# Norms between the stages of a two-layer block: the row root from a folded sum, a seed and a Newton step

## The reference, cut to what matters

```
def rms_norm(x, w):
    x32 = x.astype(f32)
    y = x32 * lax.rsqrt(jnp.mean(x32 * x32, axis=-1, keepdims=True) + EPS)
    return (y * w.astype(f32)).astype(x.dtype)
```

## Time and profile before

| what | value |
|---|---|
| time, median of 3 runs | 2105.26 us (2105.2 to 2106.39) |
| span of the profiled execution, first to last instruction | 2104.1 us |
| PE busy | 2035.2 us, 97% |
| DVE busy | 1180.8 us, 56% |
| ACT busy | 779.2 us, 37% |
| mean granted TensorE clock | 0.989 of full speed |
| table loads on ACT | 40, 1283 ns each |

### The profile page before, as it was taken

One profiled execution on the slowest core, in us unless ns is written; L12 is line 12 of the kernel. 1 busy time (PEld: TensorE's weight loads), 2 busy tenths in 40 slices (PEclk: granted clock), 3 DMA queues, 4 the chain that ended last, 5 costly groups with the idle time before them and its releaser, 6 DMA issues.

```text
span 2104.1 us, 22893 instructions
## 1 busy us (share of the span) xinstructions
PE 2035.2 (97%) x9218; PEld 1570.5 (75%) x9218; DVE 1180.8 (56%) x1851; ACT 779.2 (37%) x1063; POOL 0.2 (0%) x4
## 2 busy tenths in 40 slices
PE   5999999899999998999999999999999999999997
PEld 3567666688888875657888888787877777888886
DVE  4224545575666467865756654456776855343434
ACT  4564444542322341154322323434343445232232
POOL 0000000000000000000000000000000000000000
PEclk9999979999999999999999999999999999999999
DMA  6112211145545314422555452211111122222221
GB/s 228 53 40 81 95 66 41 50 160 200 200 173 201 126 67 135 142 66 70 200 200 200 181 212 86 97 73 61 61 60 45 57 100 81 100 96 89 100 76 40
DMA packets 41345, 232.10 MB, mean 110 GB/s; under 512 B 6100, under 2 KB 7028, under 8 KB 15512
## 3 DMA queue, kind: packets, MB, share of 16 engines
q1 hardware_dynamic: 40856, 230.09, 29.8%
q10 hardware_dynamic: 384, 0.55, 0.1%
HBM read 219.84 MB, written 2.11 MB: 105 GB/s over the span
## 4 chain that ended last, share of the span: by engine, by line
PE 90%; DVE 5%; ACT 3%; issue 1%; DMA 0%; SPq 0%; DVEq 0%; ACTq 0%
PE ps L650 23%; PE ps L652 22%; PE ps L651 22%; PE ps L1108 2%; PE ps L698 2%; PE ps L861 2%; PE ps L883 2%; PE ps L1013 2%; PE ps L1141 1%; PE ps L683 1%; PE ps L687 1%; PE ps L867 1%; PE ps L684 1%; ACT L135 1%; PE ps L1129 1%
## 5 line engine op out<-in xcount | busy, mean ns | idle before, releaser
L650 PE MATMUL ps<-hh,wh 128*128 128x512 f32 x1378 | 561.7, 408 | 13.6 <-DVE hl L1821 5.1
L652 PE MATMUL ps<-hh,wl 128*128 128x512 f32 x1378 | 539.8, 392 | 0.0
L651 PE MATMUL ps<-hl,wh 128*128 128x512 f32 x1378 | 539.5, 392 | 0.0
L1792 DVE TENSOR_TENSOR wl<-raw,wh 128x2048 fp32r<-128x2048 f32 (+2 forms) x188 | 342.8, 1827 | 158.3 <-ACT wh L139 158.3
L139 ACT ACTIVATE wh<-raw 128x2048 fp32r<-128x2048 f32 (+2 forms) x168 | 284.7, 1698 | 329.0 <-PE ps L652 251.3
L650 PEld LDWEIGHTS ps<-hh,wh 128*128 128x128 f32 x1378 | 260.0, 189 | 86.2 <-issue 30.5
L652 PEld LDWEIGHTS ps<-hh,wl 128*128 128x128 f32 x1378 | 259.3, 188 | 56.6
L651 PEld LDWEIGHTS ps<-hl,wh 128*128 128x128 f32 x1378 | 259.9, 189 | 52.4 <-issue 3.4
L1848 DVE SCALAR_TENSOR_TENSOR xT<-ps,mod,xT 128x512 f32<-128x512 f32 x80 | 59.7, 749 | 161.2 <-PE ps L652 156.0
L652 PE MATMUL ps<-ffnHh,wl 128*128 128x512 f32 x256 | 99.6, 389 | 0.0
L652 PE MATMUL ps<-m0Hh,wl 128*128 128x512 f32 x256 | 99.6, 389 | 0.0
(11 more groups left out here) (369 smaller groups left out, 2725.9 us busy)
## 6 DMA issues: line engine op xcount, KB each, us to landing
raw<-in_m SPq DMA_DIRECT2D x64, 1024.0 KB, 4.9
raw<-in_ada SPq DMA_DIRECT2D x48, 1024.0 KB, 4.7
raw<-in_ffn SPq DMA_DIRECT2D x32, 1024.0 KB, 6.9
raw<-in_hin SPq DMA_DIRECT2D x20, 1024.0 KB, 4.8
raw<-in_win SPq DMA_DIRECT2D x11, 1024.0 KB, 6.6
raw<-in_cin SPq DMA_DIRECT2D x8, 1024.0 KB, 4.8
cus<-cu SPq DMA_DIRECT2D x112, 66.0 KB, 2.0
xT<-in_xT SPq DMA_DIRECT2D x16, 256.0 KB, 4.5
```

Source lines behind the costliest of these rows:

```text
L650: pe.e.matmul(out, wh[:, k, c], xh(k), start=i == 0, stop=False)
L651: pe.e.matmul(out, wh[:, k, c], xl(k), start=False, stop=False)
L652: t = pe.e.matmul(out, wl[:, k, c], xh(k), start=False, stop=i == n - 1)
L1792: t = dve.e.tensor_tensor(P.WL[p % NSPLIT][:, k, :], P.raw[n % NRAW][:, k, :], P.WH[p % NSPLIT][:, k, :].bitcast(F32), ALU.subtract)
```

## The change

The row sum and the root are computed in another layout, in all seven norms.

- Sum: in place of one 128x128 stationary of ones and 512 moving columns, four matmuls with 32 columns of ones each take 128 tokens each. Group g writes PSUM partitions 32g to 32g+31. The 512 sums then lie in 128 columns of the bank, tokens 128g to 128g+127 in band g. This is done for `nrm_acc` and again for the last square.
- Root: ACT takes a seed, `Abs_reciprocal_sqrt` of the 128 columns, into SBUF. DVE does a Newton step on it in three instructions of 128 columns, waiting for its own result between them. No Exp and no switch of the table stand in the norm; the table of `Abs_reciprocal_sqrt` takes the places where Ln's was loaded ahead.
- Spread: PE multiplies, four times, a stationary of 128x128 made of one column of `pick` (the factor -0.5/D in the first row of a band), read with stride 0, with the 128 columns. The result, the root on all partitions for 512 tokens, goes to bank 6.
- DVE's eight products read the root from that PSUM bank in place of `R` in SBUF.
- The six idle matmuls become two between the sum and the spread, and three after the spread.
- The first half of the early split is moved: on ACT to behind the seed, on DVE to behind the Newton step.
- SP's waits for the root or for `xn` become waits for the new semaphores at the same points.

```
 def pe_row_sum(pe, P, name):
-    Z, n = P.Z, NU[name] + 1
+    Z, n = P.Z, NU[name]
     b, before = P.banks.claim_mm(("row", name))
     pe.wait_ge(Z.evac[b], before)
-    pe.wait_ge(Z.acc, 6 * n)
-    pe.e.matmul(P.PS[b][:, :], P.ones, P.acc[:, :], start=True, stop=False)
-    pe.wait_ge(Z.sq, 8 * n)
-    pe.e.matmul(P.PS[b][:, :], P.ones, P.sq[1][:, :], start=False, stop=True).then_inc(Z.full[b], 1)
+    def fold(x, first):
+        for g in range(4):
+            t = pe.e.matmul(P.PS[b][32 * g:32 * g + 32, 0:128], P.ones[:, 0:32], x[:, 128 * g:128 * g + 128], start=first,
+                            stop=not first)
+        return t
+    pe.wait_ge(Z.acc, 6 * n + 6)
+    fold(P.acc, True)
+    pe.wait_ge(Z.sq, 8 * n + 8)
+    fold(P.sq[1], False).then_inc(Z.full[b], 1)
     if name in FIRST:
-        pe_idle(pe, P, name, 7, 6)
+        pe_idle(pe, P, (name, 0), 7, 2)
+    b, before = P.banks.claim(("root", name), 6)
+    pe.wait_ge(Z.evac[b], before)
+    pe.wait_ge(Z.pick, 1)
+    pe.wait_ge(Z.root, n + 1)
+    for g in range(4):
+        t = pe.e.matmul(P.PS[b][:, 128 * g:128 * g + 128], wide(P.pick[:, g:g + 1], [0, 128]), P.fold[2], start=True,
+                        stop=True)
+    t.then_inc(Z.full[b], 1)
+    if name in FIRST:
+        pe_idle(pe, P, (name, 1), 7, 3)
...
 def act_row_rsqrt(act, P, name):
     key = ("row", name)
     act.wait_ge(*P.banks.full(key))
-    act_rsqrt_of(act, P, key, 128, 1024)
+    act.act(P.fold[0], P.PS[P.banks.bank(key)][:, 0:128], ACT.Abs_reciprocal_sqrt, scale=1.0 / D,
+            bias=P.epst[:, :]).then_inc(P.Z.seed, 1)
...
 def act_norm(act, P, name, shift=None):
+    act_row_rsqrt(act, P, name)
     if name in P.early:
         act_split(act, P, P.early[name], 0)
-    act_row_rsqrt(act, P, name)
...
+def dve_root(dve, P, name):
+    Z, key = P.Z, ("row", name)
+    b = P.banks.bank(key)
+    seed, two, out = P.fold
+    stt = dve.e.scalar_tensor_tensor
+    dve.wait_ge(Z.seed, NU[name] + 1)
+    dve.did(stt(two, P.PS[b][:, 0:128], D * EPS, seed, ALU.add, ALU.mult))
+    dve.settle()
+    dve.e.tensor_tensor(two, two, seed, ALU.mult).then_inc(Z.evac[b], 1)
+    dve.wait_ge(*P.banks.evac(key))
+    stt(out, two, -3.0 * D, seed, ALU.add, ALU.mult).then_inc(Z.root, 1)
+    if name in P.early:
+        dve_split(dve, P, P.early[name], 0)
+    key = ("root", name)
+    dve.wait_ge(*P.banks.full(key))
+    return P.PS[P.banks.bank(key)][:, :], Z.evac[P.banks.bank(key)]
...
 def dve_norm(dve, P, name, gain, shift=None):
-    if name in P.early:
-        dve_split(dve, P, P.early[name], 0)
-    dve.wait_ge(Z.rs, RS[name])
+    root, free = dve_root(dve, P, name)
     for c in range(KC):
-        dve.e.scalar_tensor_tensor(P.sq[c % 2][:, :], P.xT[:, c, :], gain(c), P.R[:, :], ALU.mult,
-                                   ALU.mult).then_inc(Z.xn, 1)
+        t = dve.e.scalar_tensor_tensor(P.sq[c % 2][:, :], P.xT[:, c, :], gain(c), root, ALU.mult, ALU.mult)
+        t.then_inc(Z.xn if c < 7 else free, 1)
...
     dve_split(dve, P, 0)
     dve.wait_ge(Z.con, 32)
+    dve.e.tensor_scalar(P.pick[:, :], wide(P.ident[:, 0:1], [32, 4]), -0.5 / D, None, ALU.mult, ALU.bypass).then_inc(Z.pick, 1)
     dve_norm(dve, P, "mix", lambda c: V(P, "n1", c))
```

More of the change, by code:

```diff
@@ L23 @@
 TABLES = {ACT.Exp: "exp_and_others", ACT.Ln: "natural_log",
-          ACT.Sigmoid: "sigmoid_and_others", ACT.Silu: "silu_and_others"}
+          ACT.Abs_reciprocal_sqrt: "abs_reciprocal_sqrt_and_small", ACT.Sigmoid: "sigmoid_and_others", ACT.Silu: "silu_and_others"}
 NRAW = 4
@@ L337 @@
 RS = {n: i + 1 for i, n in enumerate((
-    "mix", "ffn", "conv", "var", "m0", "hgrn", "sc0", "sc4", "y7", "m1", "final"))}
+    "var", "sc0", "sc4", "y7"))}
 NU = {"mix": 0, "ffn": 1, "conv": 2, "m0": 3, "hgrn": 4, "m1": 5, "final": 6}
@@ L404, in allocate @@
         "values_half", "hout_used", "qsig", "f", "w", "gsig", "ds", "up", "os", "ns", "y7", "lbd", "lb", "sw"))
-    Z.xo, Z.eps = sem("x_out"), sem("eps")
+    Z.xo, Z.eps, Z.seed, Z.root, Z.pick = (sem(n) for n in ("x_out", "eps", "seed", "root", "pick"))
     P.xT = sb("xT", [128, KC, S])
@@ L418, in allocate @@
     P.R = sb("R", [128, S])
+    P.fold = [P.R[:, 128 * i:128 * i + 128] for i in range(3)]
+    P.pick = sb("pick", [128, 4])
     P.ident, P.ones, P.bd = P.con[:, 0:128], P.con[:, 128:256], P.con[:, 256:384]
@@ L1282, in act_norm @@
     Z = P.Z
+    act_row_rsqrt(act, P, name)
     if name in P.early:
         act_split(act, P, P.early[name], 0)
-    act_row_rsqrt(act, P, name)
     for c in range(KC):
-        act.wait_ge(Z.xn, 8 * NU[name] + c + 1)
+        act.wait_ge(*((Z.xn, 7 * NU[name] + c + 1) if c < 7 else P.banks.evac(("root", name))))
         x, h = P.sq[c % 2][:, :], P.hh[:, c, :]
@@ L1310, in act_ffn @@
         act.act(F.cb[:, :], F.cb[:, :], ACT.Silu).then_inc(Z.cond, 1)
-    act.load_table(ACT.Ln)
+    act.load_table(ACT.Abs_reciprocal_sqrt)
     for s in FFN_STEPS:
@@ L2397, in vector_program @@
     dve_ffn(dve, P, "m1", "final", lambda c: mcol(P, 1, 5, c))
-    dve.wait_ge(Z.rs, RS["final"])
+    root, _ = dve_root(dve, P, "final")
     for c in range(KC):
         x = P.xT[:, c, :]
-        dve.e.scalar_tensor_tensor(x, x, V(P, "fg", c), P.R[:, :], ALU.mult, ALU.mult).then_inc(Z.xo, 1)
+        dve.e.scalar_tensor_tensor(x, x, V(P, "fg", c), root, ALU.mult, ALU.mult).then_inc(Z.xo, 1)
 def sync_program(e, P):
@@ L2451, in sync_program @@
     dma(M.mc[:, 384:512], con("mc", 128)).then_inc(Z.mla, 16)
-    sp.wait_ge(Z.xn, 8)
+    sp.wait_ge(*banks.evac(("root", "mix")))
     dma(M.cs, con("cos", 2 * S)).then_inc(Z.mla, 16)
@@ L2474, in sync_program @@
         if P.slabs[n - NRAW] == ("cin", 1):
-            sp.wait_ge(Z.rs, RS["conv"])
+            sp.wait_ge(Z.root, NU["conv"] + 1)
             dma(C.wv[:, :, :, :], a["wv"]).then_inc(Z.taps, 16)
@@ L2481, in sync_program @@
         if P.slabs[n - NRAW] == ("hin", 1):
-            sp.wait_ge(Z.rs, RS["hgrn"])
+            sp.wait_ge(Z.root, NU["hgrn"] + 1)
             dma(H.msk[:, :, :], a["msk"]).then_inc(Z.mask, 16)
```

## The result

The changed kernel takes 2120.61 us (median of 4 runs, 2119.2 to 2121.63) against 2105.82 us for the kernel before on the same chip: a ratio of 1.0069, 95% interval 1.0056 to 1.0081. I had forecast 2102.0 and a range up to 2106.0. It is slower by 14.8 us, with the interval clear of 1, and the profiled execution has a span of 2117.4 us against 2104.1.

The account below looks back on a forecast made before the run. PE, busy 97% of the span, was taken to bound the kernel, gains coming only where it waits on the norms. Gains of 3.9 us less 0.6 in mix, net 3.3 from 2105.26, gave 2102.0 us; range 2099.0 to 2106.0.

Parts of the forecast that it names:

- forecast for ffn 0.3 gained: ffn's norm: PE's products start 5.1 us behind the last row sum in place of 5.39, gaining 0.3.
- conv and m0, 0.6 each: Norms of conv and m0: chain from row sum to DVE's first product falls from 3.83 to 3.22 us.
- hgrn 0.6, m1 1.2, together 1.8: hgrn's norm: chain from 3.83 to 3.22 us; m1's, with both sums on the path, from 4.66 to 3.47.
- final, 0.6: The final norm: chain from row sum to DVE's first product falls from 3.83 to 3.22 us.
- mix was to lose 0.6: mix's norm: `pick` and Newton step wait for DVE's split; DVE's product 0.8 us later, taken as 0.6 lost.
- the three idle matmuls: Behind the spread: they hold PE 2.0 us, to 5.1, so PE starts 0.25 late, unhidden in ffn.
- The folded sums didn't queue: Rival, all norms: narrow sums run one after another, each costing 0.6 us more; 2106.4 us, chance 0.12.
- mix didn't keep its clock: Rival, mix: the spread's work spares the half-clock stretch, up to 2.6 us come back; 2099.4 us, chance 0.14.
- No load stayed: Rival, all seven norms: a table load stays on each path, 9 us more; 2111 us, chance 0.04.
- Net 3.3 us ... 2102.0: Whole kernel: 3.9 us gained in six norms, 0.6 lost in mix, taken from the median 2105.26.
- The prediction's own sign for this case: DVE's product 0.6 us earlier in each norm without the time following: the chain's far end was read wrongly.
- a falling clock: Rival, norms other than mix: PE's idling halves the clock, 2.6 us a fall; five give 2115 us, chance 0.05.

Follow-up runs that it names:

- e10: e1 plus seven idle products filling PE's 2.97 us wait ahead of conv's third projection; 2102.33 us, ratio 0.9978 to the kernel before.
- e1: Changed kernel with `pick` in the unused bytes behind `epst`, so no other tile moves; 2105.07 us, ratio 0.9994 to the kernel before.
- e2: Kernel before plus one unused 32-byte-per-partition tile behind `R`, shifting later tiles; 2124.2 us, ratio 1.0086.
- e5: Kernel before with `Hl` moved 32 bytes in m0, `r` and `rs` 32 bytes in m1, nothing in ffn; 2112.22 us.
- e8: Kernel before, unchanged, run again for a second profile; 2105.95 us.
- e6: Kernel before with `Hh` and `Hl` moved 64 bytes in ffn, 32 in m0, 128 in m1; 2120.06 us.
- e7: e1 plus four idle matmuls ahead of ffn's and m1's first sum, three between the sums of conv, m0, hgrn; 2108.36 us, ratio 1.0006.
- e11: Kernel before plus the same seven idle products ahead of conv's third projection as e10; 2107.03 us, ratio 1.0003.
- e9: No reference computation: PE alone streams zeros for 19 placements of moving and weight tiles; 389 ns a product unmoved, 395 with moving operands 32 bytes off.

## Why the prediction was wrong

**What it said of the norms held.** In e10, whose tiles lie as before, the stretches differ from the kernel before by -0.7 (forecast for ffn 0.3 gained), -0.4 and -0.7 (conv and m0, 0.6 each), -1.4 and -0.6 (hgrn 0.6, m1 1.2, together 1.8), -0.7 (final, 0.6), and +0.9 up to ffn's sum, where mix was to lose 0.6. The net is 3.5 us of span against 3.3. The closeness is partly luck, since the fill costs e10 up to 1.1 us in conv. ffn gained more than I allowed, because the three idle matmuls hold PE for less than I took, and in mix the chain lost 0.4 and not 0.8: `pick` hid beside the split's end, and the Newton step took 0.93 (20.20 to 21.13) where I had 1.28 for both. Of the 0.9 another 0.2 lies ahead of mix's first sum (17.21 us against 17.00). What else was lost up to ffn's sum I haven't followed up; that part has several stretches at half clock, and they shift from run to run.

**The rivals.** The folded sums didn't queue (0.43). mix didn't keep its clock: its spread ran at half speed (2.05 for what takes 1.13 in ffn), and its products started 0.43 apart until 30 us. No load stayed; there are 32 in place of 40. In the changed kernel's profile the clock didn't fall inside the norms after mix, but at 392.1, 801.7 and 825.6 us, for 3.4 us each. In e1's it did fall at a norm, ffn's, at 411.6. The norms' idle time isn't needed for such a fall: e2 and e5, with the norms of before, have it at 410.8 and 410.7. Whether it makes one likelier, no run shows.

**The step that failed** is "Net 3.3 us ... 2102.0": a sum over the norms taken for a sum over the program. I counted `pick` as an instruction of 0.2 us in mix and never as a tile. Its 32 bytes moved `Hh` and `Hl` away from the distance, a multiple of 256 bytes, that they had to the weight tiles. That is 768 x 3 products at 6.8 ns more from start to start, 15.6 us, nearly five times the forecast gain. The sum has a term for each instruction added and none for each allocation added. The prediction's own sign for this case, DVE's product earlier and the time not following, was to mean that I had read the far end of the chain wrongly. That sign was wrong too: e10's stretches show the far end read rightly, and the time went elsewhere.

**A second term was missing.** Even with the tiles in place (e1) the time was 2105.07 and not 2102. e1's profile has falls of the clock that e8's lacks, and the longest is the one at the wait in conv. I had listed a falling clock as a rival, but at the norms, with a chance of 0.05; one came at ffn's norm, and the longest 30 us behind conv's (767.6 to 797), at a wait that the change doesn't touch. What tips it, when the same wait of 2.97 us passes without a fall in e8, stays open: in e2 to e6, with the norms of before, the clock fell near 800 too. In e10, where the wait is filled, the profile has no fall there, and over 11 runs each the mean clock is 0.9896 against e1's 0.9870; how much of the time that one fall explains stays open, as said.

## What to carry to other kernels

Print the tiles' addresses before and after a change and compare them: a new tile, here of 16 bytes, moves what is allocated behind it, and of the distances tried here between a product's operand and its weights only multiples of 256 bytes were free. Put small tiles last, or into the unused bytes of others, and if a group of untouched products has another mean after a change, look at addresses before engines. For a gain of a few microseconds look at the clock as well: where two kernels differ in it, fill the wait behind which it fell in both of them, and time them again. See in the timeline that the fill ends before what it waits for comes; in e7, e10 and e11 it didn't.

## What the runs showed of the hardware

Products of 128x128 weights and 512 columns, issued one behind the other, start every 0.227 us where operand and weights are a multiple of 256 bytes apart, and every 0.233 us where they are 32 bytes off (21.76 and 22.40 us for the 96 products of L407 and L409 of e9, from start to start); 128 bytes off it is 0.232. I had expected a start aligned to 32 bytes to be as good as any other. The same wait of 2.97 us was followed by 6 us of half clock in e1 and by none in e8.
